# Sums of a stick-breaking attention split into rounded halves, with a mask added by a product and some vector work reordered

## What is computed

```
mask = kpos[None, :] < qpos[:, None]
z = einsum('bhqd,bhkd->bhqk', q, k) * scale
log_beta = log_sigmoid(z)
log_rem = where(mask, log_sigmoid(-z), 0.0)
after = cumsum(log_rem, axis=key, reverse=True) - log_rem
a = where(mask, exp(log_beta + after), 0.0)
o = einsum('bhqk,bhkd->bhqd', a, v)
```

## Time and profile before

| | |
|---|---|
| median of three runs | 1506.97 us |
| the profiled execution | 1510.53 us, of which its span is 1508.7 us |
| TensorE matmul | 1386.1 us busy, 92% of the span |
| VectorE | 789.6 us, 52% |
| ScalarE | 595.5 us, 39% |
| GpSimd | 14.7 us, 1% |
| 16 DMA engines | 372.42 MB read, 248 GB/s over the span |

### The profile page before, as it was taken

One profiled execution on the slowest core, in us unless ns is written; L12 is line 12 of the kernel. 1 busy time (PEld: TensorE's weight loads), 2 busy tenths in 40 slices (PEclk: granted clock), 3 DMA queues, 4 the chain that ended last, 5 costly groups with the idle time before them and its releaser, 6 DMA issues.

```text
span 1508.7 us, 23588 instructions
## 1 busy us (share of the span) xinstructions
PE 1386.1 (92%) x10389; PEld 1153.4 (76%) x10389; DVE 789.6 (52%) x1110; ACT 595.5 (39%) x743; POOL 14.7 (1%) x32
## 2 busy tenths in 40 slices
PE   8999999998777777767899999999999999999998
PEld 6898898854334333433689899999999989999986
DVE  6655867411011101100688887666467687865653
ACT  4554555311000000100446865444344586544443
POOL 0000000000000000000010000000001000000000
PEclk9999999999898888979999999999999999999999
DMA  9553348899999999999764436555536434555640
GB/s 314 178 172 113 111 169 327 321 427 426 427 427 427 427 427 427 426 427 423 288 186 148 168 121 194 188 170 200 218 113 196 168 113 167 168 183 179 230 176 28
DMA packets 117406, 377.13 MB, mean 250 GB/s; under 512 B 8215, under 2 KB 53623, under 8 KB 104759
## 3 DMA queue, kind: packets, MB, share of 16 engines
q1 hardware_dynamic: 115879, 371.52, 64.4%
q0 software_dynamic: 1424, 4.08, 1.0%
HBM read 372.42 MB, written 1.06 MB: 248 GB/s over the span
## 4 chain that ended last, share of the span: by engine, by line
PE 70%; DMA 21%; DVE 5%; ACT 2%; issue 1%; SPq 1%; POOL 0%; ACTq 0%; DVEq 0%
PE bank L653 34%; DMA SZ<-in_w_exp_up 8%; DMA ring<-in_w_exp_up 6%; PE bank L914 5%; PE bank L675 4%; PE bank L1285 4%; PE bank L1279 4%; PE bank L705 3%; PE bank L1087 3%; DMA SZ<-in_w_exp_down 3%; DMA tail_hn<-in_w_exp_up 3%; PE bank L1117 2%; DVE parts L1826 2%; PE bank L1040 1%; DMA ring<-in_w_ckv 1%
## 5 line engine op out<-in xcount | busy, mean ns | idle before, releaser
L1826 DVE TENSOR_TENSOR parts<-ring,parts 128x2048 fp32r<-128x2048 f32 x155 | 349.6, 2287 | 99.4 <-ACT parts L1375 98.2
L653 PE MATMUL bank<-hnr,parts 128*128 128x256 f32 x2784 | 342.0, 285 | 1.9 <-DVE parts L1826 1.9
L653 PEld LDWEIGHTS bank<-hnr,parts 128*128 128x128 f32 x2784 | 337.2, 193 | 5.5 <-issue 2.9
L1375 ACT ACTIVATE parts<-ring 128x2048 fp32r<-128x2048 f32 x152 | 282.3, 1904 | 94.9 <-PE bank L1285 29.2
L653 PE MATMUL bank<-SKr,parts 128*128 128x256 f32 x1824 | 227.3, 284 | 2.6 <-DVE parts L1826 2.6
L653 PEld LDWEIGHTS bank<-SKr,parts 128*128 128x128 f32 x1824 | 221.0, 192 | 5.5 <-issue 2.6
L1087 PE MATMUL bank<-ring,TMP 128*32 128x512 f32 x576 | 81.4, 716 | 45.3 <-DMA ring<-in_w_exp_up 45.3
L2224 DVE COPY KV<-bank 128x256 f32<-128x256 f32 x16 | 6.8, 425 | 216.2 <-PE bank L1067 216.2
L1087 PEld LDWEIGHTS bank<-ring,TMP 128*32 128x32 f32 x576 | 22.0, 127 | 97.7 <-issue 82.7
L1551 ACT ACTIVATE TMP<-bank 128x512 f32<-128x512 f32 x15 | 9.0, 597 | 161.1 <-PE bank L1040 161.1
L914 PE MATMUL bank<-Gr,parts 128*128 128x256 f32 x576 | 69.9, 283 | 0.0
(11 more groups left out here) (385 smaller groups left out, 1854.2 us busy)
## 6 DMA issues: line engine op xcount, KB each, us to landing
ring<-in_w_in SPq DMA_DIRECT2D x60, 1024.0 KB, 7.3
ring<-in_w_ffn_in SPq DMA_DIRECT2D x44, 1024.0 KB, 7.3
ring<-in_w_exp_gate SPq DMA_DIRECT2D x18, 2048.0 KB, 38.7
ring<-in_w_exp_up SPq DMA_DIRECT2D x18, 2048.0 KB, 43.2
ring<-in_w_exp_down SPq DMA_DIRECT2D x18, 2048.0 KB, 39.0
ring<-in_w_ffn_out SPq DMA_DIRECT2D x20, 1024.0 KB, 6.0
G<-in_w_exp_gate SPq DMA_DIRECT2D x7, 2048.0 KB, 38.3
SZ<-in_w_exp_up SPq DMA_DIRECT2D x7, 2048.0 KB, 43.2
```

Of the source, the lines that this page charges most:

```text
L653: m = mm(b(name)[:, T * half:T * half + T], part(chunk, ws)[:, k, P * mt:P * mt + P], src[xs][:, k, :], start=k == 0 and i == 0, stop=k == ...
L1375: A(parts[:, 2 * (r % 2), 2048 * i:2048 * i + 2048], ring[:, CHUNK[chunk][0], 2048 * i:2048 * i + 2048], ACT.Copy).then_inc(high_made, 1)
L1826: v.tensor_tensor(parts[:, 2 * (r % 2) + 1, at], ring[:, CHUNK[chunk][0], at], parts[:, 2 * (r % 2), at].bitcast(F32), ALU.subtract).then_ ...
```

## The change

`sb_after_sum` no longer multiplies in plain f32. VectorE copies the masked log_rem to a high part rounded to fp32r (`rem_parts`), GpSimd subtracts it from log_rem to make the low part (semaphore sb_low), and TensorE forms for each of the two parts one product of 384 columns with the triangle and one of 128 columns with ones. Two further products of 128 columns, identity times a table with -1e30 wherever the key isn't before the query, add the mask into the same bank, so that the exponential is zero there; `sb_mask` and its semaphore are gone and `sb_out` waits for the exponential. Four rounded tables are made once, in layer 0, on VectorE. For heads 0 and 1 the copy also waits until the turn of the other attention's head 2 or 3 is done.

The order is changed in six places: TensorE computes `sb_after_sum(0)` after the second half tile of ga1 instead of between the two, and that of heads 1, 2, 4 and 6 after one gate half tile; VectorE makes the second low half of ga1 before the sum of head 0 is added instead of after the mask, takes the gates of a head in the same turn of the loop instead of in the next (heads 0 to 5), and, in the first block, makes the second low half of zm1 at head 5 before the norm and the gate product instead of after them. The list in `group_plan` keeps its order.

```
--- before
+++ after
@@ -132,9 +132,7 @@
                 s += [f"bz{h + 2}", f"bz{h + 3}"]
-            if h < 7:
-                s += [f"ba{h + 1}"]
-            s += [name for name, half in GATE_HALVES[h] if half == 0]
+            s += [f"ba{h + 1}"] * (h < 7) + [name for name, half in GATE_HALVES[h] if half == 0]
             if h == 0:
@@ -222,6 +220,7 @@
         cnt = sb("cnt", [P, 1], I32)
+        below = sb("below", [P, 256], F32R)
 
@@ -348,6 +347,9 @@
         lamt = view(KV, 1536, LAYERS * 4, 64)
+        rem_parts = [(SKr[:, 4096 + 384 * i:4096 + 384 * i + 384], SKr[:, 4864 + 384 * i:4864 + 384 * i + 384]) for i in range(2)]
+        ident_r, below_r = below[:, 0:128], below[:, 128:256]
+        earlier_r, ones_r = SKr[:, 5888:6016], SKr[:, 6016:6144]
         y_out = view(G, 0, TB, D)
@@ -388,13 +390,14 @@
         y_gained, y_first, y_second = sem("y_gained"), sem("y_first_half"), sem("y_second_half")
+        sb_low, tables_rounded = sem("sb_low"), sem("tables_rounded")
         still, low_rank_blank = sem("filler_ready"), sem("low_rank_blank")
...
         blank, passed, iota_moved = sem("blank"), sem("passed"), sem("iota_moved")
-        sb_logs, sb_rem, sb_exp, sb_prob = (sem(n) for n in ("sb_logs", "sb_rem", "sb_exp", "sb_prob"))
+        sb_logs, sb_rem, sb_exp = (sem(n) for n in ("sb_logs", "sb_rem", "sb_exp"))
         lam_sums, lam_exps, out_done = sem("lam_sums"), sem("lam_exps"), sem("out_done")
@@ -614,6 +617,10 @@
                     swap_halves(dk_turned[:, 2 * j:2 * j + 2], dk[:, 2 * j:2 * j + 2], turned_in[f"dk{j}"])
+                for h in range(8):
+                    high_part, low_part = rem_parts[h % 2]
+                    pool.wait_ge(sb_rem, 8 * l + h + 1)
+                    nc.gpsimd.tensor_tensor(low_part, lrem[h % 2], high_part.bitcast(F32), ALU.subtract).then_inc(sb_low, 1)
 
@@ -1213,17 +1220,20 @@
                     room(pe, name)
+                    pe.wait_ge(tables_rounded, 1)
                     pe.wait_ge(sb_rem, 8 * l + h + 1)
-                    lr = lrem[h % 2]
-                    mm(b(name)[:, 0:T], earlier, lr[:, 0:T], start=True, stop=False)
-                    mm(b(name)[:, P:T], ones, lr[:, T:T + P], start=False, stop=True)
-                    m = mm(b(name)[:, T:T + P], earlier, lr[:, T:T + P], start=True, stop=True)
+                    pe.wait_ge(sb_low, 8 * l + h + 1)
+                    for i, lr in enumerate(rem_parts[h % 2]):
+                        mm(b(name)[:, 0:384], earlier_r, lr, start=i == 0, stop=False, skip_group_check=True)
+                        mm(b(name)[:, P:T], ones_r, lr[:, T:T + P], start=False, stop=False, skip_group_check=True)
+                    mm(b(name)[:, 0:P], ident_r, below_r, start=False, stop=False, skip_group_check=True)
+                    m = mm(b(name)[:, T:T + P], ident_r, below_r, start=False, stop=True, skip_group_check=True)
                     fin(m, name)
...
                         room(pe, f"bo{h // 2}{x}")
-                    pe.wait_ge(sb_prob, 8 * l + h + 1)
+                    pe.wait_ge(sb_exp, 8 * l + h + 1)
                     causal_out(f"bo{h // 2}{x}", stick[h % 4], bv, 64 * h, 64, 64 * (h % 2), h % 2 == 1)
@@ -1235,18 +1245,20 @@
                 split_tile("ga0" + x, z_parts, "ga1" + x, 2)
+                split_tile("ga0" + x, z_parts, "ga1" + x, 3)
                 sb_after_sum(0)
-                split_tile("ga0" + x, z_parts, "ga1" + x, 3)
                 diff_out(3)
...
                         sb_scores(h + 3)
-                    if h < 7:
+                    if h in (2, 4, 6):
                         sb_after_sum(h + 1)
-                    for name, half in GATE_HALVES[h]:
+                    for i, (name, half) in enumerate(GATE_HALVES[h]):
                         j = int(name[2])
                         split_tile(f"{name[:2]}{j // 2}{x}", z_parts, name + x, 2 * (j % 2) + half)
+                        if i == 0 and h in (0, 1, 3, 5):
+                            sb_after_sum(h + 1)
                     if h == 0:
@@ -2025,6 +2037,8 @@
                     moba_logits(h + 2)
+                if h == 5:
+                    low("zm1", [1])
                 if h < 6:
@@ -2032,7 +2046,7 @@
                     v.tensor_tensor(og, og, rg, ALU.mult).then_inc(og_ready, 1)
-                if h < 6:
+                if h < 5:
                     low("zm0" if h < 4 else "zm1", [h % 2])
@@ -2306,6 +2320,10 @@
                     dve.wait_ge(lam_exps, 1)
+                    v.tensor_copy(earlier_r, earlier)
+                    v.tensor_copy(ones_r, ones)
+                    v.tensor_copy(ident_r, ident)
+                    v.tensor_scalar(below_r, later, -1.0, BIG, ALU.add, ALU.mult).then_inc(tables_rounded, 1)
                 link(v.tensor_tensor(lam[:, l:l + 1], lam_e[:, 2 * l:2 * l + 1], lam_e[:, 2 * l + 1:2 * l + 2], ALU.subtract))
@@ -2372,16 +2390,15 @@
                     emptied(dve, name)
-                    v.tensor_tensor(diagonals(lr), diagonals(lr), diagonals(strict), ALU.mult).then_inc(sb_rem, 1)
+                    link(v.tensor_tensor(diagonals(lr), diagonals(lr), diagonals(strict), ALU.mult))
+                    if h < 2:
+                        full(dve, f"dt{2 + h}{x}")
+                    v.tensor_copy(rem_parts[h % 2][0], lr).then_inc(sb_rem, 1)
 
...
                     freed(v.tensor_tensor(lbeta[h % 2], b(name)[:, 0:384], lbeta[h % 2], ALU.add), name)
-
-                def sb_mask(h):
-                    dve.wait_ge(sb_exp, 8 * l + h + 1)
-                    v.tensor_tensor(diagonals(stick[h % 4]), diagonals(stick[h % 4]), diagonals(strict), ALU.mult).then_inc(sb_prob, 1)
 
@@ -2424,9 +2441,8 @@
                 sb_logs_of(1)
+                low("ga1" + x, [1])
                 sb_add(0)
-                sb_mask(0)
-                low("ga1" + x, [1])
                 take_scaled("ga1" + x, two(ga, 1), by_attn)
@@ -2434,9 +2450,6 @@
                         sb_add(h + 1)
-                        if h:
-                            gates_of(h - 1)
-                        sb_mask(h + 1)
                     if h in (2, 4, 6):
@@ -2444,6 +2457,8 @@
                         sb_logs_of(h + 3)
+                    if h < 6:
+                        gates_of(h)
                     if h < 2:
```

## The result

The kernel after takes 1515.58 us (median of six runs, 1514.69 to 1516.81); the kernel before took 1508.26 in the same series. The ratio is 1.0048, 95% interval 1.0037 to 1.0059, so +7.3 us where +4.6 was forecast. The profiled execution took 1516.81 us, its span 1514.6, 5.9 more than the span before.

A forecast was written before the change was run, and what follows sets the result against it. The prediction took TensorE's work to bound the head loop, with VectorE and ScalarE nearly full. Two layers at +3.1 us less 1.6 at zm1 gave +4.6, from 1506.97 to 1511.6 us; 8-in-10 range 1502.5 to 1519.5.

The forecast's parts named there:

- The bound: Head loop: TensorE's work bounds; VectorE 86% and ScalarE 80% full; work put before a chain link emerges at its end.
- Part 1: First block: zm1's low half made earlier removes TensorE's 1.60 us wait; -1.6 us taken, bounds -1.6 to 0.
- rival D: Change hardly felt, zm1's gain swallowed in the experts: 1513.2 us; chance 0.35 shared with forecast and its slow-product end.
- Part 2: Tables, made once: four vector instructions, at most 0.35 us each, covered by VectorE's idle time: 0, or 1.4 uncovered.
- Part 3: Each head's sum on TensorE: 1.14 us instead of 0.90, +0.24 a head, +1.9 a layer (ends +0.3, +3.5).
- rival C: Faster: ScalarE's delay never reaches head 2, a sum costs 0.74 us, old waits go: 1501.9 us; chance 0.14.
- Part 4: Head loop chain: head 0's exponential 3.0 us later, TensorE waits 1.4 at head 2's sum; layer +3.1 with sums.
- The merge: End of each layer's head loop: VectorE 3.5 us later, TensorE 3.1, slack about 1, so no wait: 0.
- Rival A: Head loop: GpSimd and VectorE hold each other up; 1515.8 us, or 1532.6 with a slow subtract; chance 0.25.
- The sum: Whole kernel: +6.2 us for two layers less 1.6 at zm1, +4.6, giving 1511.6 us on the median.

The follow-up runs named there:

- e3: Kernel after, but ScalarE makes both high halves of gb0 before the exponential of head 0; ratio to the kernel before 0.9999.
- e4: Kernel after, but VectorE adds the sum of head 0 before the second low half of ga1; ratio to the kernel before 1.0012.
- zm1_only: Kernel before, with only the second low half of zm1 made at head 5 ahead of the norm and gate product; ratio 0.9993.
- e2: Kernel before with all six order moves alone, f32 sums and VectorE masks kept, nothing on GpSimd; ratio 1.0045.
- e7: Kernel after, but ga3 and the sum of head 2 exchange banks in the list; ratio to the kernel before 1.0046.
- e5b: e3 with the low part of log_rem made by VectorE instead of GpSimd; ratio to the kernel before 1.0045.
- e8_again: Repeat run of e3 plus two pieces of VectorE's work moved to where it stood idle; 1505.02 us, ratio to the kernel before 0.9981.
- e6: Kernel after, but TensorE computes the sum of head 2 ahead of ga3's first half tile; ratio to the kernel before 1.0095.
- e1: Kernel after with every order move undone, leaving the split sums, GpSimd's low parts and the mask as a product; ratio to before 1.0041.

## Why the prediction came out as it did

**The bound, right.** That front work comes out later at the end of the chain was the main matter: by one exchange each, e3 undoes the loss and e4 three quarters of it. The two stretches are equal to 0.01 us.

**Part 1, half right.** The wait of 1.60 went as computed (low half made by 177.19 + 2.28 = 179.5, in a run in which VectorE is 1.25 later at this place than in the earlier trace rows; forecast 178.3). Next late are the probabilities of head 6, which the working didn't look at: they were hidden by that same wait before. The waits give 0.77, not 1.6; whether the experts gave that back, as rival D has it, zm1_only leaves open.

**Part 2, right.** The four instructions take 0.55 us of VectorE, its idle time before the take falls from 2.36 to 1.82, and TensorE has no new wait there (1.04 and 0.44 where it had 0.93 and 0.45).

**Part 3, mis-sized, and in sign.** A sum was forecast at 1.14 us (+0.24). From a sum's first product to the next work, the 16 sums add up to 14.12 us before and 13.23 after, 0.83 each (-0.06). With the f32 sums in the moved order (e2) a sum takes 0.91. Two things in the forecast's 1.14 were wrong. The 0.14 "at the change of type" is the time from the start of the old sum's last product to the next work (1214.31 to 1214.45); it holds that product itself and was no extra. And the products of 128 columns were put at 0.165: the two behind one of 384 columns take 0.06 (1231.71 to 1231.77), under the lowest bound of 0.065, and the two of the mask 0.11 to 0.12 (1232.05 to 1232.17), as the row of 64 columns had it. Against that, the second product of 384 columns takes 0.23 and not 0.17. A sum with a half tile right behind it comes to 0.74 or 0.75, the number that rival C had. Over a layer this is -0.45 us where +1.9 stood.

**Part 4, the chain, right to 0.2 us.** Taking off 2.62: the exponential of head 0 at 1216.1 (forecast 1216.1), VectorE's first log step of head 2 at 1224.7 (1224.8), copy 0.36 (0.34), GpSimd's subtract for head 2 1.27 (1.1), the wait at ga1 0.48 (0.5). The step that failed is "now one half tile stands in front" of head 2's sum: that half tile can't run as cover, since its bank is the one that held head 2's scores, and that bank is freed by head 2's second log step, the delayed chain itself. TensorE waits 2.43 there instead of 1.4 at the sum. e7 gives the half tile another bank, and the wait stands at the sum with 1.63. The working read the half tile's operands and left its output bank out. The prediction named as a sign that it is wrong that TensorE has no wait at head 2: at the sum of head 2 there is none, and the wait stands one half tile ahead of it, on the same chain.

**The merge, wrong.** That "the merge finds them in time" (0) was argued from VectorE +3.5, TensorE +3.1 and a slack of 1. Measured: VectorE's part before the merge starts at 1271.31 - 2.62 = 1268.7, 4.25 later than before, and TensorE comes 2.3 later, as its products were cheaper. Of the 4.25, 3.15 go with e3's exchange, so they are the delayed chain; where the remaining 1.10 come from isn't shown (GpSimd beside VectorE stretches some instructions, but e2 has nothing on GpSimd and is later still, 4.52). So the layer's number is luck: against the forecast the products came out some 2.3 us a layer cheaper, and the waits some 2.3 dearer (ga3 2.43 for 1.4, the merge 1.00 for 0, the sum of head 6 0.27 for 0). Both errors cancel, and the layer came out at +3.33 for +3.1.

**Rival A, in the trace but not in the time.** The subtract takes 3.00 us when it starts with a low part of VectorE (1216.09 against 1215.92), and low parts take 2.72 instead of 2.28 when they start during a subtract. The long subtract ends 0.9 us after the low part, about its length alone. The Trainium skill's rule (SBUF — State Buffer, section Who interferes with whom) agrees in kind with this: the one that comes second waits. The sign that the prediction named, a subtract that starts more than 0.3 us after the copy's end, isn't there (0.08 us): the hold shows in the lengths, not in the starts. What rival A made of the time doesn't follow: the waits of 1.7 at head 2 and 1.0 at head 6 are not there (0.27 at the latter), and e2 and e5b say that GpSimd isn't the main cost. That its 1515.8 lies nearer to the measured 1515.6 than the forecast's 1511.6 is chance.

**The sum.** The span is 5.9 longer, and comes together so: at the start of the first stretch +0.33 (814.85 against 814.52), +3.33 in it, -1.04 between the stretches (two waits for low parts of 0.29 and 0.45 at 1158 in the kernel before aren't there after), +3.33, and nothing behind. Of the 0.77 of the first block nothing is seen at 814 us: this run also had a wait of 2.02 us at 36 us, far ahead of the change, where the profiled run of before has 0.49 and most others 0.5 to 0.8 or none (e8_again has 2.02 too). On the medians it is +7.3 where the spans have 5.9 and the forecast 4.6; single runs scatter by 2 us. The forecast's absolute number, 1511.6, is 4.0 under the measured one, 1.3 of it because the kernel before itself stood at 1508.26 in this series and not at 1506.97.

## What to carry to other kernels

When work is put in front of a link as cover, walk its output bank as well as its operands: cover that needs a buffer freed by the delayed chain is no cover. When a vector instruction is moved ahead, look at what the next engine has queued behind the instruction that it delays; here 3.7 us of unrelated copies stood behind a delayed exponential, and one exchanged pair of lines was worth 7 us. Before a won wait is counted, look which engine sets the end of the stretch: in e7 it was another, and nothing was won. And a change can be sound and still lose: measure it again with the orders around it repaired before it is thrown away.

## What the runs showed of the hardware

- A wait of TensorE can cost more than its length. Behind 4.69 us of idleness in e6 the clock was granted at 0.50 (1.2 GHz) for 6 us in the first layer and 3.7 us in the second. After shorter waits it fell in one layer and not in the other, with the same instructions: e7 after 1.63 (second layer only, TensorE 1.6 us slower, which later waits took up), e1 after 1.86 (first layer only: its stretches are 73.22 and 71.73), e5b after 2.11 before the merge (first only, to 0.51 over 3 us). Behind the 2.43 in the kernel after and the 2.21 in e2 it stayed at 1.00 in both layers. What decides in the short cases these traces don't show.
- GpSimd subtracts 128 by 384 f32 in 1.01 us where no vector instruction with two operands from SBUF is under way at its start, and in 1.27 where a short one is; behind a long one that started 0.17 earlier it took 3.00. Beside such a subtract VectorE's 128 by 2048 goes from 2.28 up to 2.72, its 128 by 256 from 0.43 up to 0.54.
- In fp32r, in the kernel after, within a sum a product of 384 columns is followed by the next after 0.17 to 0.28 us and one of 128 columns by the next after 0.06 to 0.12.
